# DeltaNet: a second, permuted copy of the block inverses in DRAM in place of four transposes per chunk

## The reference, cut to what matters

```python
lower = jnp.where(strict, beta[..., :, None] * kk * decay, 0.0)
rhs = jnp.concatenate([v * beta[..., None], k * (beta * jnp.exp(g_cum))[..., None]], axis=-1)
sol = lax.linalg.triangular_solve(lower, rhs, left_side=True, lower=True, unit_diagonal=True)
```

## Time and profile before

| | before |
|---|---|
| time, median of 3 runs | 1634.82 us (1634.08 to 1636.33) |
| span of the profiled execution | 1634.9 us |
| that execution's own time | not listed apart; its span lies inside the three runs |
| TensorE matmul busy | 1604.4 us (98%) |
| VectorE, ScalarE, GpSimd busy | 56%, 39%, 16% |
| DMA | 223.05 MB, mean 136 GB/s |

### The profile page before, as it was taken

One profiled execution on the slowest core, in us unless ns is written; L12 is line 12 of the kernel. 1 busy time (PEld: TensorE's weight loads), 2 busy tenths in 40 slices (PEclk: granted clock), 3 DMA queues, 4 the chain that ended last, 5 costly groups with the idle time before them and its releaser, 6 DMA issues.

```text
span 1634.9 us, 23987 instructions
## 1 busy us (share of the span) xinstructions
PE 1604.4 (98%) x8239; PEld 1313.7 (80%) x8239; DVE 909.5 (56%) x1440; ACT 640.9 (39%) x1313; POOL 260.3 (16%) x282
## 2 busy tenths in 40 slices
PE   6999999999999999999999999999999999999998
PEld 5687878888877777878788888788888888888886
DVE  4576655435545454546652489766666666334424
ACT  4334456555544444444212244333333333232413
POOL 1036561011101010100000003223322220000000
PEclk9999999999999999999999999999999999999999
DMA  8826666655733333523545322322222224543412
GB/s 282 276 91 215 202 199 186 201 182 153 227 99 110 98 109 98 161 88 111 168 142 193 109 59 65 111 82 77 77 77 87 92 71 146 213 176 130 148 45 103
DMA packets 223678, 223.05 MB, mean 136 GB/s; under 512 B 19066, under 2 KB 189187, under 8 KB 223619
## 3 DMA queue, kind: packets, MB, share of 16 engines
q1 hardware_dynamic: 216642, 197.12, 37.7%
q0 software_dynamic: 6976, 25.17, 4.0%
HBM read 163.53 MB, written 60.31 MB: 137 GB/s over the span
## 4 chain that ended last, share of the span: by engine, by line
PE 87%; DVE 4%; DMA 3%; POOL 3%; SPq 1%; issue 1%; ACT 1%; DVEq 0%; POOLq 0%; ACTq 0%
PE pm L1642 22%; PE pm L1656 15%; PE ps L1211 13%; PE pd L1501 11%; PE pm L1211 8%; PE pm L1596 3%; PE sc L1454 2%; PE tT L1477 2%; PE tT L1466 2%; PE pm L1554 1%; POOL pr L1124 1%; POOL Xi L1126 1%; PE gps L1391 1%; DMA adab<-in_w_ada_dram 1%; DVE est L2311 1%
## 5 line engine op out<-in xcount | busy, mean ns | idle before, releaser
L1211 PE MATMUL ps<-act_hi,w_hi 128*128 128x512 f32 x448 | 150.0, 416 | 2.6 <-DVE est L2316 1.7
L2225 DVE TENSOR_TENSOR w_lo<-w_raw,w_hi 128x1024 fp32r<-128x1024 f32 x60 | 77.4, 1290 | 123.0 <-ACT w_hi L1751 113.2
L1211 PE MATMUL ps<-act_lo,w_hi 128*128 128x512 f32 x448 | 138.9, 391 | 0.0
L1211 PE MATMUL ps<-act_hi,w_lo 128*128 128x512 f32 x448 | 138.5, 390 | 0.0
L1656 PE MATMUL pm<-act_hi,w_hi 128*128 128x512 f32 x352 | 137.2, 390 | 0.0
L1656 PE MATMUL pm<-act_hi,w_lo 128*128 128x512 f32 x352 | 137.0, 389 | 0.0
L1656 PE MATMUL pm<-act_lo,w_hi 128*128 128x512 f32 x352 | 136.9, 389 | 0.0
L1642 PE MATMUL pm<-act_hi,w_hi 128*128 128x512 f32 x320 | 124.5, 389 | 0.0
L1642 PE MATMUL pm<-act_lo,w_hi 128*128 128x512 f32 x320 | 124.5, 389 | 0.0
L1642 PE MATMUL pm<-act_hi,w_lo 128*128 128x512 f32 x320 | 124.5, 389 | 0.0
L1501 PE MATMUL pd<-act_hi,w_hi 128*128 128x512 f32 x256 | 111.3, 435 | 0.0
(11 more groups left out here) (375 smaller groups left out, 3462.0 us busy)
## 6 DMA issues: line engine op xcount, KB each, us to landing
w_raw<-in_w_in_dram SPq DMA_DIRECT2D x44, 512.0 KB, 5.3
w_raw<-in_w_ffn_in_dram SPq DMA_DIRECT2D x44, 512.0 KB, 3.7
h_raw<-h_d SPq DMA_DIRECT2D x36, 512.0 KB, 3.4
a_raw<-in_w_ada_dram SPq DMA_DIRECT2D x32, 512.0 KB, 4.2
w_raw<-in_w_ffn_out_dram SPq DMA_DIRECT2D x44, 256.0 KB, 3.8
h_d<-hid SPq DMA_DIRECT2D x21, 512.0 KB, 2.7
pk_d<-pk SPq DMA_DIRECT2D x8, 768.0 KB, 3.7
qkva_d<-est POOLq DMA_DIRECT2D x12, 512.0 KB, 6.0
```

Of the source, the lines that this page charges most:

```text
L1211: ins = pe.matmul(dst[:, cols], wt[:, ds % 2, k, :], at[:, cols], start=(first and n == 0), stop=(last and n == 2))
L2225: dve.tensor_tensor(w_lo[:, ds % 2], w_raw[:, ds % NR], w_hi[:, ds % 2].bitcast(F32), ALU.subtract)\
```

## The change

After the solve GpSimd copies `Xi` with rows and columns of each block exchanged into `LB`, which nobody needs any more. SyncE stores it in a new `invT_d`, waits for both stores, and loads for each chunk four more DMAs, the diagonal blocks of `UmT`, ahead of those of `Um`. `UmT` takes the place of `junk` and is set to zero by one more memset on GpSimd; squares go to `om` or `zt`. Step `Q_T0` is gone with its copy, the steps behind it move two slots forward, and the wait for the inverse moves to `Q_Y5`. In phase B `ast_free[0]` is given one slot later.

```diff
@@ names, steps @@
+        invT_d = dram("invT_d", [NT, NBLK, BLK, BLK])
-            Um, St, junk = (b1(n) for n in ("Um", "St", "junk"))
+            Um, St, UmT = (b1(n) for n in ("Um", "St", "UmT"))
-        (Q_TO, Q_GQ, Q_QS, Q_KS, Q_TV, Q_T0, Q_Y5, Q_U6, Q_Z, Q_W, Q_V, Q_AY, Q_KY) = range(13)
-        NQ = 13
+        (Q_TO, Q_GQ, Q_QS, Q_KS, Q_TV, Q_Y5, Q_U6, Q_Z, Q_W, Q_V, Q_AY, Q_KY) = range(12)
+        NQ = 12
@@ SyncE: load_inverse, projection_a @@
                 for d in range(P // BLK):
+                    sp.dma_start(diagonal(UmT, d), diagonal_d(invT_d, t, d)).then_inc(inv_in, 16)
+                for d in range(P // BLK):
                     sp.dma_start(diagonal(Um, d), diagonal_d(inv_d, t, d)).then_inc(inv_in, 16)
...
-                    sp.wait_ge(xi_zero, 3)
+                    sp.wait_ge(xi_zero, 4)
                     sp.wait_ge(xi_ready, 1)
                     sp.dma_start(inv_d.rearrange("t b c r -> (t b) (c r)"), Xi[:, :, :].rearrange("p c r -> p (c r)"))\
                         .then_inc(inv_stored, 16)
-                    sp.wait_ge(inv_stored, 16)
+                    sp.wait_ge(xi_ready, 2)
+                    sp.dma_start(invT_d.rearrange("t b c r -> (t b) (c r)"), LB[:, :, :].rearrange("p c r -> p (c r)"))\
+                        .then_inc(inv_stored, 16)
+                    sp.wait_ge(inv_stored, 32)
                     load_inverse(0)
@@ GpSimd @@
             pool.memset(Um[:, :], 0.0).then_inc(xi_zero, 1)
+            pool.wait_ge(ext_stored, 16)
+            pool.memset(UmT[:, :], 0.0).then_inc(xi_zero, 1)
             pool.memset(Xi[:, :, :], 0.0).then_inc(xi_zero, 1)
-            pool.wait_ge(xi_zero, 2)
+            pool.wait_ge(xi_zero, 3)
...
-            pool.wait_ge(xi_zero, 3)
+            pool.wait_ge(xi_zero, 4)
             pool.wait_ge(low_in, 16)
             solve(range(BLK - 1))
+            pool.wait_ge(xi_ready, 1)
+            pool.tensor_copy(LB[:, :, :], Xi[:, :, :].rearrange("p c r -> p r c")).then_inc(xi_ready, 1)
@@ TensorE: gdn_step, attention_slot @@
-                elif q == Q_T0:
-                    pe.wait_ge(inv_in, t * 64 + 64)
-                    for h in range(B_H):
-                        ins = pe.transpose(hd(gps, h), hd(Um, h), ident[:, :])
                 elif q == Q_Y5:
+                    pe.wait_ge(inv_in, t * 128 + 128)
                     pe.wait_ge(ct_ready, t * 2 + 1)
                     for h in range(B_H):
-                        ins = pe.matmul(hd(gps, h), Ct[:, 0, h * P:(h + 1) * P], hd(Tm, h), start=True, stop=True)
+                        ins = pe.matmul(hd(gps, h), Ct[:, 0, h * P:(h + 1) * P], hd(UmT, h), start=True, stop=True)
...
-                                if kt == 0 and (j, e) == (6, 0):
+                                if kt == 0 and (j, e) == (6, 1):
                                     ins.then_inc(ast_free[0], 1)
@@ ScalarE: squares to om (two places) or zt (one), gdn_read_act @@
-                    act.activation(hd(junk, h), hd(pk[:, t % 4, 0], h), ACT.Square, accum_out=ssq[:, 0, t, h:h + 1])\
+                    act.activation(hd(om, h), hd(pk[:, t % 4, 0], h), ACT.Square, accum_out=ssq[:, 0, t, h:h + 1])\
...
-                dst = {Q_TV: vn, Q_T0: Tm, Q_Y5: Tm, Q_Z: zt, Q_W: Tm}.get(q)
+                dst = {Q_TV: vn, Q_Y5: Tm, Q_Z: zt, Q_W: Tm}.get(q)
```

More of the change, by code:

```diff
@@ L1819, in query_squares @@
                 for h in range(B_H):
-                    ins = act.activation(hd(junk, h), hd((gps, aT)[e], h), ACT.Square,
+                    ins = act.activation(hd(om, h), hd((gps, aT)[e], h), ACT.Square,
                                          accum_out=ssq[:, 1, t, h:h + 1])
@@ L1870, in gdn_read_act @@
                     for h in range(B_H):
-                        act.activation(hd(junk, h), hd(om, h), ACT.Square, accum_out=sso[:, h:h + 1])\
+                        act.activation(hd(zt, h), hd(om, h), ACT.Square, accum_out=sso[:, h:h + 1])\
                             .then_inc(sso_ready, 1)
```

## The result

The changed kernel takes 1639.66 us (median of 8 runs, 1636.92 to 1644.29). The kernel before, timed on the same chips beside it, takes 1635.43 us (8 runs, 1634.08 to 1636.45). The ratio is 1.0028, with a 95% interval of 1.0019 to 1.0037: slower by 4.2 us between the medians, by 4.6 us going by the ratio. The forecast was 1636.6 us, range 1633.6 to 1639.6. The sign was right. The measured median is 3.1 us above the forecast and lies just above the range. Of these 3.1 us, 0.6 belong to the kernel before, which stood at 1634.82 us when the forecast was made and at 1635.43 here; the rest is the change, forecast at +1.8 us.

A forecast was written before the change was run, and what follows sets the result against it. TensorE, busy 1604.4 of 1634.9 us, was taken as the bound. Memset +0.4, chunk 0 +3.2, chunks 1 to 3 +0.6 and transposes of seven chunks -2.45 gave +1.8 on 1634.82: 1636.6 us, range 1633.6 to 1639.6.

The forecast's parts named there:

- The clock: TensorE's granted clock, read as 1.00 over its 3.9 us wait; nothing counted for it in a stall of that length.
- The waits for `zt`: Chunks 1 to 3: `Q_W` waits 0.2 us each for `zt` behind block 4's scaling; +0.6 us, bounds 0 and +1.8.
- the removal: Transposes of `Um` gone from TensorE: 0.35 us per chunk, -2.45 us for seven chunks, chunk 0's counted separately.
- Chunk 0's chain: Chunk 0: copy 1.3 us, second store +1.6, four more load issues +1.8, delaying block 3 and `Q_U6`; chunk total +3.2 us.
- The 0.4 us for `zt` in chunk 0: Chunk 0: block 4 loads late, so `zt` comes after `Q_W` is due; +0.4 us, bounds 0 and 1.
- The upper bound of chunk 0: Most that chunk 0 was said to cost: +5.8 us, beside a forecast of +3.2 and a lower bound of +2.0.
- The memset: Clearing `UmT` on GpSimd lies on the path to `L1340`'s wait: +0.4 us, between -0.5 and +0.5.
- Rival 1: Chunk 0: copy of 2.6 us, second store landing 4.23 us later, loads issued at full-queue rate; 1639.0 us, 17 in 100.
- Rival 2: Port contention between VectorE and GpSimd spreads around the copy; 1637.8 us, or 1639.3; 8 in 100 for the slower end.
- Rival 3: Chunk 0 costs nothing because block 3's data come by the time TensorE is due; 1631.5 us, 5 in 100.

The follow-up runs named there:

- fillers in phase C: Kernel before, with 14 matmuls of no use put into TensorE's 3.9 us wait in phase C: 1632.93 us, ratio 0.9989.
- the removal alone: Kernel before without the transposes and their copy, later steps two slots forward, no second copy, store, memset or loads; computes another product: 1633.66 us, ratio 0.9992.
- VectorE's wait in place: Changed kernel in which VectorE makes the low part of the weights in chunk 0 only after GpSimd's second copy is written: 1638.39 us, ratio 1.0015.
- `zt` first: Changed kernel in which ScalarE copies `zt` before it scales column block 4, in all four chunks of phase A: 1638.67 us, ratio 1.0021.
- the five moves: Changed kernel with block 3 before the stores' wait, `UmT` cleared late, `zt` copied before scaling, 14 idle phase C matmuls, VectorE waiting for the copy: 1629.90 us, 0.9965.
- block 3 first: Changed kernel with chunk 0's column block 3 loaded behind the second store, ahead of the wait for both stores: 1635.92 us, ratio 1.0009.

## Why the prediction was off, by its own steps

**The clock: the step that failed.** The sentence was "TensorE's clock was granted at 1.00 ... over the stretch that holds its 3.9 us wait. I count nothing for it in a stall of the same length." It cost 1.6 us in chunk 0 of the profile, the whole of what makes chunk 0 dearer than forecast and more. It was a stretch that ended at the wrong place: the earlier trace rows stop 0.15 us behind the end of the wait, and the half clock stands in the windows behind it. Rows of matmuls would have shown it too: 0.43 us apart there, and 0.23 elsewhere. The runs with fillers in phase C show cause and price; those in chunk 0 show the same in their profiles.

**The waits for `zt`: a term as wrong in size as the clock, and the removal mis-sized too.** The term was +0.6 for three chunks; they cost 1.00 + 0.78 + 0.60 = 2.4. The forecast let block 4 land when it did before. After the change ScalarE first waits 2.4 us for raw weights (to 303.86) and then for block 4 (to 305.62, in the earlier trace rows 301.51). Chunk 1 begins 3.3 us later itself, so block 4 is 0.8 us late against its chunk. Where these transfers lost their time was not tried one by one. The run of the removal alone, with 1.7 us of `zt` waits, shows that the four loads more per chunk are not needed for there to be such waits. Against that stands a removal that is worth more than the 0.35 us taken from two starts in the earlier trace rows: 0.48 in phase A, 0.41 in phase B. For seven chunks that is 3.1 in place of 2.45.

**Chunk 0's chain: right in its course, with errors that cancelled.** Copy 2.08 instead of 1.3; the second store landed 5.3 us after the solve, where the first alone took 4.2, so +1.0 instead of +1.6; four issues more +1.9 instead of 1.8; block 3 took 4.9 us to land instead of 3.9. `Q_U6` came 0.4 us later after the solve than forecast. The two waits are 3.2 us, the forecast had 3.6. The 0.4 us for `zt` in chunk 0 did not occur. The upper bound of chunk 0 was added up too low: by its own terms (+1.0, +1.4 and +0.6 over the +3.2) it is +6.2, not +5.8. The 1.5 us by which the Trainium skill (GPSIMD Engine Reference, Elementwise — side-by-side cycle accounting) led to estimate the copy is a best case there; the same section has about 2.6 cycles of 1.2 GHz per element for a two-operand loop, and with that the copy would be estimated at 2.2 us. The measured 2.08 us is nearer to this, though the copy has one operand.

**What the base was.** The prediction sets the span of 1634.9 us beside the median time of 1634.82. But a time is longer than its span, by 1.6 to 1.7 us in most of the runs (1637.33 and 1635.7) and by 2.7 in the profiled one of after. So that span belongs to an execution of about 1636.5 us. The forecast adds its sum to the median, so this changes nothing in it.

**The memset: right.** +0.42 between the scores and chunk 0, and the wait is 1.1 us again when it is moved.

**Rival 1** (the list dearer, 1639.0 us) has the right size by another way: `Q_U6` started only 0.4 us later than forecast, not 1.5, and the loads came at the rate of an empty queue. **Rival 2** had the right mechanism: "only if GpSimd is itself held, by one 1.2 us instruction, does the copy's end move". It is held, by 0.9 us, when VectorE begins first; the forecast gave it 8 in 100, while three of nine profiles with the copy show it, together with the late solve. The price is not only the 0.9 us but also the clock behind the longer wait.

**The spread.** How much of the 7.4 us between the times of after the late solve and the long copy explain is open: with VectorE's wait in place 4.2 us are left. What the times do go with is the granted clock of the whole execution: it is 0.997 or 0.998 in the four shortest executions of after and 0.994 in the longest. Stretches of half clock come and go in other places too: seven of the fifteen profiles have one or two in their first 40 us, both kernels' among them, and in phase C two profiles (the removal alone, `zt` first) have the clock at 0.50 from inside the 3.9 us wait on, for over 6 us and not for some 3, and lost 2.7 to 2.8 us there.

**Rival 3** (nothing lost in chunk 0) did not occur in the changed kernel; with the five moves chunk 0 takes 57.45 us, about as long as before.

**How it adds up.** In the two profiles: 1.6 of clock, 2.8 of longer waits in chunk 0 (3.2 against 0.5), 2.4 of waits for `zt`, 0.4 of memset, less 3.5 of transposes in eight chunks; that is 3.7 of the 4.0 us measured. A few tenths in chunk 0 (one is a new 0.2 us wait of the one-column matmul for `asc`) are left. What lies between these 4.0 us and the 4.6 of the ratio is not shown; executions with the late solve and the long copy, of which the profile after is none, can be part of it. How often they occur outside the nine profiles was not measured.

Against the forecast of 1.8 us the two profiles have 2.2 us more: 1.6 for the clock and 1.8 for the waits for `zt` in chunks 1 to 3, less 0.8 for the removal and 0.7 for the waits of chunk 0, and the few tenths that are left.

## What to carry to other kernels

A wait of TensorE is priced with what follows it: look at the granted clock of the microseconds behind the longest waits of the kernel before, not of those up to their end. Then a stall of 2.6 us is one of 4.2, and a few idle matmuls in a long wait can be worth about as much as the work that a change saves (1.8 us in phase C, 1.3 us for the removal alone).

When transposes are replaced by a transfer, look first at what stands in one list behind the transfer. Here the column block behind eight loads cost more than all transposes, and to load it ahead of the wait for the stores gave 3 us back.

When the long instructions of two engines meet, a shift of less than 1 us between them can lengthen the one on the path (here 0.65 us behind against 0.09 us ahead). Look at more than one profile before you price it, and at what else has moved: here the solve was late in the same executions. To let the engine with slack wait is worth a try; here its gain was within the overlap of the intervals.

## What the hardware showed unexpectedly

- The clock fell to 0.50 behind waits of 1.8 to 3.9 us in chunk 0 and phase C (1.8, 1.9, 2.0, 2.3, 2.4, 2.6, 3.9) and stayed at 1.00 behind those of 0.3 to 1.1 us in chunk 0. In chunk 0 it stayed down for some 3 us, and cost about 1.6 us each time; in phase C it cost 1.6 us in ten profiles and 2.7 to 2.8 in two. The length of a wait alone does not decide: in the first 40 us of the profile with block 3 first a wait of 1.9 us was followed by 1.00, and in that of after the clock fell to 0.50 at 19 us, about two waits of 1.1 us that end at 17.2 and 19.4 us.
- GpSimd's permuted copy of 128x1024 f32 took 2.1 us and VectorE's two-input subtraction of 128x1024 next to it 2.5, or 3.0 and 1.2, after which of them began first. The later one was held each time. Alone, behind the copy, the subtraction took 1.23 us.
- An edit that only adds work to an engine (14 matmuls of 128 columns) shortened the kernel by 1.8 us. One that only adds a wait (VectorE) went with a median 1.3 us lower, which the intervals do not secure.
